# Four raw weight buffers, one down-projection buffer and a gather that skips padding rows in the experts of a two-layer decoder

## The reference, cut to what matters

```python
    gi = jnp.argmax(lg, axis=-1)
    ...
    top_p, top_i = lax.top_k(jax.nn.softmax(le, axis=-1), TOP_K)
    gate = p_top * top_p / jnp.sum(top_p, axis=-1, keepdims=True)
    ...
    def run_block(args):
        xb, e = args
        hid = jax.nn.silu(xb @ w_gate[e]) * (xb @ w_up[e])
        return hid @ w_down[e]
    ...
    y = jax.ops.segment_sum(out[dest] * sw[:, None], stok, num_segments=T)
```

## Time and profile before

| | |
|---|---|
| median of 3 runs | 3122.04 us (3121.51 to 3127.49) |
| profiled execution | 3119.75 us, span 3117.8 us |
| granted TensorE clock, mean | 0.936 of full speed |
| expert stage of layer 0, first to last gate/up product | 496.9 us, 47 blocks |
| expert stage of layer 1, the same | 485.1 us, 46 blocks |

### The profile page before, as it was taken

How to read it: one execution, slowest core, us unless ns; L and a number is a source line. 1 busy time by engine, 2 the same in 40 slices (tenths; PEclk the granted TensorE clock), 3 DMA queues, 4 the chain that set the end, 5 groups by cost and what they waited for, 6 DMA issues and landing times. The chain is left out here.

```text
span 3117.8 us, 48627 instructions
## 1 busy us (share of the span) xinstructions
PE 2673.4 (86%) x15109; PEld 2236.8 (72%) x15112; DVE 1747.1 (56%) x3154; ACT 1260.4 (40%) x2369; POOL 724.0 (23%) x923
## 2 busy tenths in 40 slices
PE   5999979997968947998898599799879947989997
PEld 4999958875847836777676488578658836767775
DVE  4222246665755665667765366588733354676664
ACT  3222132225841104556654222288611104675653
POOL 1000023321110002444343143211100002444433
PEclk9999989998988968999999799899979968999998
DMA  6111112215536516899997322222154415999995
GB/s 243 50 56 52 40 60 78 75 65 165 163 121 234 194 61 216 261 301 302 316 281 228 118 87 80 91 83 88 53 198 143 149 39 179 298 359 285 283 308 132
DMA packets 175389, 509.57 MB, mean 163 GB/s; under 512 B 53800, under 2 KB 81456, under 8 KB 150320
## 3 DMA queue, kind: packets, MB, share of 16 engines
q1 hardware_dynamic: 142480, 393.69, 34.7%
q0 software_dynamic: 32800, 114.51, 15.4%
HBM read 374.56 MB, written 133.56 MB: 163 GB/s over the span
## 5 line engine op out<-in xcount | busy, mean ns | idle before, releaser
L1700 DVE TENSOR_TENSOR moe_parts<-expert_w,moe_parts 128x1024 fp32r<-128x1024 f32 x384 | 452.3, 1221 | 238.4 <-ACT moe_parts L1649 234.9
L1582 PE MATMUL ps<-moe_parts,moe_xT 128*128 128x512 f32 x2232 | 551.6, 403 | 23.0 <-issue 16.0
L1582 PEld LDWEIGHTS ps<-moe_parts,moe_xT 128*128 128x128 f32 x2232 | 418.1, 191 | 125.3 <-issue 20.5
L1649 ACT ACTIVATE moe_parts<-expert_w 128x1024 fp32r<-128x1024 f32 x384 | 373.3, 1047 | 80.3 <-PEq L155 78.8
L1109 PE MATMUL ps<-out_w,out_catT 128*128 128x512 f32 x1344 | 322.4, 399 | 14.2 <-DVE out_w L1265 11.8
L560 PE MATMUL ps<-in_gate_w,in_gate_hnT 128*128 128x384 f32 (+1 forms) x1536 | 319.4, 367 | 7.4 <-DVE in_gate_w L679 7.4
L1582 PE MATMUL ps<-moe_parts,moe_hidT 128*128 128x512 f32 x1116 | 289.0, 408 | 26.9 <-DVE moe_hidT L1713 24.2
L560 PEld LDWEIGHTS ps<-in_gate_w,in_gate_hnT 128*128 128x128 f32 x1536 | 278.7, 190 | 37.4 <-issue 7.5
L1109 PEld LDWEIGHTS ps<-out_w,out_catT 128*128 128x128 f32 x1344 | 255.7, 192 | 69.4 <-DVE out_w L1265 12.6
L560 PE MATMUL ps<-in_qk_w,in_qk_hnT 128*128 128x512 f32 x1152 | 268.4, 394 | 9.2 <-DVE in_qk_w L679 9.2
L1582 PEld LDWEIGHTS ps<-moe_parts,moe_hidT 128*128 128x128 f32 x1116 | 205.7, 191 | 76.2 <-DVE moe_hidT L1713 32.8
(11 more groups left out here) (262 smaller groups left out, 4150.8 us busy)
## 6 DMA issues: line engine op xcount, KB each, us to landing
expert_w<-in_w_gate SPq DMA_DIRECT2D x64, 1024.0 KB
expert_w<-in_w_up SPq DMA_DIRECT2D x64, 1024.0 KB
expert_w<-in_w_down SPq DMA_DIRECT2D x64, 1024.0 KB
hn_d<-out_hn SPq DMA_DIRECT2D x32, 512.0 KB, 2.6
in_gate_xt<-in_x SPq DMA_DIRECT2D x16, 512.0 KB
in_qk_xt<-in_x SPq DMA_DIRECT2D x16, 512.0 KB
att_k<-k_d SPq DMA_DIRECT2D x64, 128.0 KB, 2.9
out_ht<-in_x SPq DMA_DIRECT2D x16, 512.0 KB, 4.6
```

Source lines behind the costliest of these rows:

```text
L1582: last = nc.tensor.matmul(out, left[:, a, k, :], right(b, k), start=(n == 0 and k == 0), stop=(n == 2 and k == K_ - 1))
L1649: nc.scalar.activation(parts[:, j, 0, at], K.expert_w[:, j, at], ACT.Copy).then_inc(w_high.sem, 1)
L1700: nc.vector.tensor_tensor(parts[:, j, 1, at], K.expert_w[:, j, at], parts[:, j, 0, at].bitcast(F32), ALU.subtract).then_inc(w_low.sem, 1)
```

## The change

- `RING` = 4 raw buffers: the two slots of `K.expert_w` and two more (`more`), with a semaphore each. Experts 2 and 3 are loaded at the start of the stage without a wait; expert e is loaded into the buffer of e - 4. w_gate waits for 2 gate/up pieces of e - 4, w_up for 4, w_down for its 2 down pieces.
- `parts` becomes `gu_parts` (two slots) and `d_parts` (one), with counters of their own. The down pieces of an expert are split at the end of its own first block, not at the end of the first block of the expert before. TensorE waits for `d_low` before every `lower`, and no longer for all pieces at the end of a first block.
- `pair` becomes `round_`: four experts are unrolled, in a loop of 6 rounds.
- The gather takes its rows from `K.where`, in which padding has a row number of 2048 or more, with a bounds check at 2047 that skips such rows. `xg` is cleared once before the first gather. `K.who` is gone.
- ScalarE reads the gate from `K.gates` directly; `set_gate` is gone.
- `w_in_odd` waits for 30 experts instead of 32.

```diff
+RING = 4
...
-            self.who = keep("who", [P, NBMAX], I32)
...
-                load_expert(K, sp, layer, e, e)
+                load_expert(K, sp, layer, e, K.expert_w[:, e, :], K.expert_in[layer][e])
...
-            own_.mark(V.tensor_copy(K.who[:, :], found[:, 1, :]))
...
-        gate = sb("gate", [P, 1])
-
-        parts = sb("parts", [P, 2, 2, EW], F32R)
+        more = sb("more", [P, RING - 2, EW])
+        ring = [K.expert_w[:, i, :] for i in range(2)] + [more[:, i, :] for i in range(RING - 2)]
+        gu_parts = sb("gu_parts", [P, 2, 2, GU], F32R)
+        d_parts = sb("d_parts", [P, 2, EW - GU], F32R)
         gathered_s, scattered_s = sem("gathered"), sem("scattered")
         who_set, where_set = Count(sem("who_set")), Count(sem("where_set"))
         x_turned, x_high, x_low = Count(sem("x_turned")), Count(sem("x_high")), Count(sem("x_low"))
-        w_high, w_low = Count(sem("w_high")), Count(sem("w_low"))
+        gu_high, gu_low, d_high, d_low = (sem(n) for n in ("gu_high", "gu_low", "d_high", "d_low"))
...
-            def pair(i, is_first, is_last):
-                for j in range(2):
-                    e = i * 2 + j
+            def round_(i, is_first, is_last):
+                for j in range(RING):
+                    e = i * RING + j
                     m0 = 0 if is_first and j == 0 else end_of(eng, e)
-                    first_block(i, j, m0, not (is_first and j == 0), not (is_last and j == 1))
+                    first_block(i, j, m0, not (is_first and j == 0), not (is_last and j == RING - 1))
                     end = end_of(eng, e + 1)
                     with eng.If(end > m0 + 1):
 
                         with eng.Fori(m0 + 1, end) as m:
-                            block(m, j)
-            pair(0, True, False)
-            with eng.Fori(1, NE // 2 - 1) as i:
-                pair(i, False, False)
-            pair(NE // 2 - 1, False, True)
+                            block(i, j, m)
+            round_(0, True, False)
+            with eng.Fori(1, NE // RING - 1) as i:
+                round_(i, False, False)
+            round_(NE // RING - 1, False, True)
...
-                load_expert(K, sp, layer, i * 2 + j, j, lambda n: alone(
-                    sp, w_low, i * (2 * PIECES) + ((j - 2) * PIECES + (n + 1) * PIECES // 3), K.tick_sp))
-            with sp.Fori(1, NE // 2) as i:
-                for j in range(2):
+                load_expert(K, sp, layer, i * RING + j, ring[j], K.expert_in[layer][j], lambda n: alone(
+                    sp, (Count(gu_low), Count(gu_low), Count(d_low))[n],
+                    ((i - 1) * RING + j) * (GU_PIECES, GU_PIECES, D_PIECES)[n] + (GU_PIECES // 2, GU_PIECES, D_PIECES)[n], K.tick_sp))
+            for j in range(2, RING):
+                load_expert(K, sp, layer, j, ring[j], K.expert_in[layer][j])
+            with sp.Fori(1, NE // RING) as i:
+                for j in range(RING):
                     load(i, j)
             if layer == 0:
 
-                sp.wait_ge(w_low.sem, NE * PIECES)
+                sp.wait_ge(gu_low, (NE - RING + 2) * GU_PIECES)
+                sp.wait_ge(d_low, (NE - RING + 2) * D_PIECES)
                 sp.dma_start(K.w_in_odd, K.x["w_in_odd"].rearrange("a (p k) n -> p (a k) n", k=DK)).then_inc(K.weights_in[5], 16)
 
         @block.gpsimd
         def _(g):
             def gather(m):
-                nc.gpsimd.tensor_copy(who[:, :], K.who[:, m:m + 1] if isinstance(m, int) else K.who[:, bass.ds(m, 1)]).then_inc(who_set.sem, 1)
+                nc.gpsimd.tensor_copy(who[:, :], K.where[:, m:m + 1] if isinstance(m, int) else K.where[:, bass.ds(m, 1)]).then_inc(who_set.sem, 1)
                 alone(g, who_set, m + 1, K.tick)
                 nc.gpsimd.indirect_dma_start(xg[:, :], None, K.hn_d[layer],
-                                             bass.IndirectOffsetOnAxis(ap=who[:, :], axis=0)).then_inc(gathered_s, 16)
-
-            def set_gate(m):
-                nc.gpsimd.tensor_copy(gate[:, :], K.gates[:, bass.ds(m, 1)]).then_inc(gated.sem, 1)
...
+            g.memset(xg[:, :], 0.0).then_inc(cleared, 1)
+            g.wait_ge(cleared, 1)
             gather(0)
...
-                set_gate(m - 1)
-
                 alone(g, x_turned, m + 2, K.tick)
                 gather(m + 2)
                 scatter(m - 1)
-            set_gate(total - 1)
...
-                pe.wait_ge(w_low.sem, i * (2 * PIECES) + j * PIECES + GU_PIECES)
+                pe.wait_ge(gu_low, i * (RING * GU_PIECES) + (j + 1) * GU_PIECES)
                 raise_(m, j)
                 turn_x(m + 1)
                 if behind:
-                    lower(m - 1, 1 - j)
-                pe.wait_ge(w_low.sem, i * (2 * PIECES) + (j + 1) * PIECES)
-                pe.sem_inc(K.tick_pe, 1)
-
-            def block_(m, j):
+                    pe.wait_ge(d_low, i * (RING * D_PIECES) + j * D_PIECES)
+                    lower(m - 1)
+
+            def block_(i, j, m):
                 turn_hid(m - 1)
                 raise_(m, j)
                 turn_x(m + 1)
-                lower(m - 1, j)
+                pe.wait_ge(d_low, i * (RING * D_PIECES) + (j + 1) * D_PIECES)
+                lower(m - 1)
             turn_x(0)
             in_turn(pe, first_block, block_)
             total = end_of(pe, NE)
             turn_hid(total - 1)
-            lower(total - 1, 1)
+            pe.wait_ge(d_low, NE * D_PIECES)
+            lower(total - 1)
...
-            def split(i, j, pieces):
-
-                for n in pieces:
+            def split_gu(i, j):
+                a.wait_ge(K.expert_in[layer][j], i * 48 + 48)
+                for n in range(GU_PIECES):
                     at = slice(n * PIECE, (n + 1) * PIECE)
-                    nc.scalar.activation(parts[:, j, 0, at], K.expert_w[:, j, at], ACT.Copy).then_inc(w_high.sem, 1)
+                    nc.scalar.activation(gu_parts[:, j % 2, 0, at], ring[j][:, at], ACT.Copy).then_inc(gu_high, 1)
+
+            def split_d(j):
+                for n in range(D_PIECES):
+                    at = slice(n * PIECE, (n + 1) * PIECE)
+                    nc.scalar.activation(d_parts[:, 0, at], ring[j][:, GU + n * PIECE:GU + (n + 1) * PIECE], ACT.Copy).then_inc(d_high, 1)
...
-                until(a, gated, m + 1)
-
                 a.wait_ge(scattered_s, m * 16 + 16)
-                nc.scalar.activation(y[:, :], yp, ACT.Copy, scale=gate[:, 0:1]).then_inc(y_out.sem, 1)
+                nc.scalar.activation(y[:, :], yp, ACT.Copy, scale=K.gates[:, bass.ds(m, 1)]).then_inc(y_out.sem, 1)
 
             def first_block(i, j, m, behind, ahead):
-                ni, nj = i + j, 1 - j
                 if ahead:
-
-                    a.wait_ge(K.expert_in[layer][nj], ni * 48 + 48)
                     if behind:
                         until(a, up, m)
-                    split(ni, nj, range(GU_PIECES))
+                    split_gu(i + (j + 1) // RING, (j + 1) % RING)
                 act(m)
                 x_out(m + 1)
                 if behind:
                     y_scaled(m - 1)
-                if ahead:
-                    split(ni, nj, range(GU_PIECES, PIECES))
-
-            def block_(m, j):
+                    split_d(j)
+
+            def block_(i, j, m):
                 act(m)
                 x_out(m + 1)
                 y_scaled(m - 1)
-            a.wait_ge(K.expert_in[layer][0], 48)
-            split(0, 0, range(PIECES))
+            split_gu(0, 0)
             x_out(0)
+            split_d(0)
...
+                ni, nj = i + (j + 1) // RING, (j + 1) % RING
                 if ahead:
-                    split(ni, nj, range(GU_PIECES // 2))
+                    split_gu(ni, nj, range(GU_PIECES // 2))
                 if behind:
                     hid_out(m - 1)
                 if ahead:
-                    split(ni, nj, range(GU_PIECES // 2, GU_PIECES))
+                    split_gu(ni, nj, range(GU_PIECES // 2, GU_PIECES))
                 hidden(m)
                 x_out(m + 1)
-                if ahead:
-                    split(ni, nj, range(GU_PIECES, PIECES))
-
-            def block_(m, j):
+                if behind:
+                    split_d(i, j)
+
+            def block_(i, j, m):
                 hid_out(m - 1)
                 hidden(m)
                 x_out(m + 1)
-            split(0, 0, range(PIECES))
+            split_gu(0, 0, range(GU_PIECES))
             x_out(0)
+            split_d(0, 0)
...
```

More of the change, by code:

```diff
@@ L175, in build @@
             self.weights_in = [self.ctx.enter_context(nc.semaphore(f"weights_in{i}")) for i in range(8)]
-            self.expert_in = [[self.ctx.enter_context(nc.semaphore(f"expert_in{l}{i}")) for i in range(2)]
+            self.expert_in = [[self.ctx.enter_context(nc.semaphore(f"expert_in{l}{i}")) for i in range(RING)]
                               for l in range(2)]
@@ L1283, in _, with load_expert @@
             log(end.plus(1))
-def load_expert(K, sp, layer, e, slot, until_free=lambda n: None):
```

(19 more changed lines are left out.)

14 lines of the change are left out of this document (7 added, 7 removed).

## The result

The changed kernel took 3162.2 us (median of 4 runs, 3155.2 to 3169.9), the kernel before 3122.3 beside it: a ratio of 1.0125, with a 95% interval of 1.0097 to 1.0152. The change makes the kernel slower by 40 us; forecast were +19 and 3139 us, inside a range of 3090 to 3172. The profiled execution took 3155.2 us with a span of 3153.5, 35.7 over that of before; it is the fastest of the four, so the trace shows 36 of the 40 us. The same stage can differ by some 10 us between the traces of two kernels whose medians agree (485 and 496 us for layer 1 in the kernel before and in `e4_shift`), so single traces are read here for mechanisms more than for their sums.

The account below looks back on a forecast made before the run. The prediction took the DMA engines, at nine tenths in the two expert stages, as the full resource. Its terms, 14 - 11 + 20 + 12 - 5 - 7 - 4 = +19 us on 3119.75, gave 3139 us, range 3090 to 3172.

Parts of the forecast that it names:

- (1): Start of each expert stage: memset, 6 MB loaded ahead of the first gather, next gathers delayed; +14 us (6 to 16).
- (2): Two-block expert after two-block expert: the 1.2 us stall goes, the gather inside the burst is short; -11 us (-13 to 0).
- (3): One-block expert after a two-block one: the gather falls behind the burst and comes late; +20 us (0 to 29).
- (4): First blocks after one-block experts, and runs of those: gathers take 8.90 us and come last; +12 us (-10 to +24).
- (5): Loop ends: rounds of four experts halve VectorE's waits before its splits; -5 us (-10 to 0).
- (6): w_in_odd load: last gather's rows all skipped, load two experts earlier meets a gather of 2 rows; -7 us (-9 to +4).
- (7): Last two experts of a layer run with no loads beside them; -4 us (-6 to 0).
- (8): Gate copies leaving GpSimd, removed table copy, single pair of w_down halves, bounds check on gathers: taken as 0.
- C: Gathers: a skipped row costs as much as a moved one; +57 us, 3177 us, chance 0.08.
- A: Gathers: the burst costs them nothing because skipped rows shorten it; -32 us, 3088 us, chance 0.25.
- D: Loop body of four experts no longer stays in the instruction store; fetches cost 54 to 107 us, about 3200, chance 0.04.
- B: Gathers behind the burst land at about 8.1 us, by turns between queues; -4 us, 3116 to 3124, chance 0.17.

Follow-up runs that it names:

- e4_shift: Kernel before with one unused tile of 224 bytes per partition ahead of the stages' tiles, shifting later addresses; 0.9993 of the kernel before.
- e3_late: Changed kernel with the loads of experts 2 and 3 held back until TensorE has turned the first block; 1.0110 of the kernel before, 3159.7 us.
- e1_paced: Changed kernel with SyncE loading in two portions, gate and up of expert e+1, then down of expert e; 3121.4 us, 0.9997 of the kernel before.
- e7_all_three: Changed kernel with two-portion loads, experts 2 and 3 held back until the first turn, and w_in_odd in four parts; 3109.2 us, 0.9946 of the kernel before.
- e2_all_rows: Changed kernel with the gather's bound above every index and hn_d 128 rows longer, so padding rows are fetched in full; 1.0173 of the kernel before.

## Why the prediction was right in its sign and half in its size

The sign and the mechanism held: the three loads go together because the wait for w_down queues gate and up behind it, the gather of the second block of a pair falls behind them, and undoing that alone returns the kernel's time. Step by step, from the table:

**(1) Start, +14: measured +14.4.** The parts were different. `e3_late` puts 4.9 us a layer on the 6 MB (4.4 were said) and leaves 2.3 for the memset and the bounds check (0.95 were said). I had also 1.5 us for the next gathers; they were not late. The chain of waits of layer 1 has the gather, for 4.51 in the earlier trace rows:

```profile
2605.96 10.26 DMA moe_xg<-hn_d,moe_who
```

**(2) Two-block behind two-block, -11: measured +2.7.** This is the step that failed. The stalls in second steps went, 127.1 to 112.7. But I called the gather issued in the burst "short", since some 25 rows of 128 are left of it. It was the gather of 50 rows, of 92 and of 2 that stalled TensorE for 2.25, 2.39 and 1.92 us, and the first steps grew from 115.1 to 132.2. A skipped row keeps its packet, and the packets have to get past the loads.

**(3) One-block behind two-block, +20: measured +31.7.** Eleven places with a stall of 1.8 us were said; of the 13 steps eleven do have one, 2.2 us each, 24.4 in all. The gather falls 3.1 us behind the first of the three issues, where I had 4.2 (my own rows give 9.53 + 1.8 - 7.54 = 3.8), and takes 9.4 us on average, not 8.9 less something for skipped rows. The other 7.3 us are what a stall does behind itself, which I hadn't counted. Columns as in the earlier trace rows: first what follows the 1.92 us stall of expert 5, then the 2.25 us one of expert 4:

```profile
1297.40:1301.30 3.90, 3.90 (x22) 3.40 (x23) 1.62 (x3) 1.03 (x1) 1.32 (x3) 1.00 0.38 77
...
1274.80:1280.30 5.50, 5.47 (x22) 4.77 (x23) 1.59 (x3) 1.02 (x1) 1.45 (x3) 0.69 0.49 95
```

The same 22 matmuls: at a granted clock of 1.00 (2.4 GHz) in 3.90 us, and at 0.69, between the levels of 2.4 and 1.2 GHz, in 5.50. A step costs its stall and 0.25 us, or its stall and 1.5 to 2.0 us: the latter in 6 of the 25 first steps behind two-block experts (and in expert 30's), all with stalls of 2.25 us or more, though one of 2.39 us cost no more than its 0.25. The granted clock goes with it: from the stall to the next product it is 0.65 to 0.73 in all seven, and 1.00 behind the stalls of 2.39, 2.17, 2.05 and 1.92 us. 6 x 1.5 = 9 us over those two kinds of step, which none of my terms had priced.

**(4) and (5) First blocks behind one-block experts, +12 and -5: measured about -5.** I said that a gather of 8.9 us would come last in the runs of one-block experts, a hair behind VectorE. It comes a hair ahead. 18 of these 33 gathers have all three loads issued in the 6 us before them, and TensorE takes them up 9.2 us behind their issue, yet hardly one stalls it: the waits fell from 21.9 to 1.5 us, and TensorE stands ahead of `lower` instead, so that the rows are there when it comes to turn them. The steps stayed at 12.0 us, since VectorE sets the pace, for which I had worked out 11.1. `lower` waits for the halves of the hidden values, which stand behind two gate/up splits:

```profile
2786.14 0.33 SPq L1293 DMA_DIRECT2D moe_more<-in_w_up  x1
...
2788.26 2.35 DVE L1700 TENSOR_TENSOR moe_gu_parts<-moe_more,moe_gu_parts 128x1024 fp32r<-128x1024 f32 x2
2788.44 3.00 PE L1582 MATMUL ps<-moe_d_parts,moe_hidT 128*128 128x512 f32 x12 [0.71 <-issue]
2789.05 1.36 POOL L1541 DMA_INDIRECT moe_xg<-hn_d,moe_who  x1 [0.89 <-POOL moe_who L1539]
...
2797.87 1.16 PE L1590 MATMUL ps<-ident,moe_xg 128*128 128x128 f32 x8
...
2799.37 0.42 DVE L1720 TENSOR_TENSOR moe_hidT<-ps,moe_hidT 128x256 fp32r<-128x256 f32 x1
2799.71 1.22 DVE L1700 TENSOR_TENSOR moe_gu_parts<-expert_w,moe_gu_parts 128x1024 fp32r<-128x1024 f32 x1
2799.90 0.47 PE L1582 MATMUL ps<-moe_d_parts,moe_hidT 128*128 128x512 f32 x1 [0.87 <-issue]
```

From `lower` to `lower` 11.46 us; the gather, 2.9 us behind the last of its three loads, is turned 8.8 us behind its issue without a stall. A gather that is no longer late gives nothing here; the waits ahead of `lower` in these 33 steps went from 22 to 48 us.

**(6) w_in_odd, -7: measured 0.** The end stall of 8.9 us is gone, and expert 30's first step grew by 9.1. I had it meet "one gather of 2 rows"; it did, and the 2 rows took 14.4 us. The same error as in (2).

**(7) Last two experts, -4: measured -1.3**, of which 0.5 is the shorter undisturbed step of (8). Their transfers had hardly been in the way before.

**(8) Gates, table, single down buffer, bounds check: 0.** No wait of `lower` for the down halves shows, and the bounds check adds 0.15 us to a gather's issue (1299 for 1154 ns on average): near nothing, but not for the first. Not foreseen: the matmuls' 3 ns (0.13 us in an undisturbed step, 12 us at most over 91 steps, all inside the sums above), and 4.0 us ahead of layer 0's stage and 2.8 between the layers, which lie within what such stretches vary from trace to trace (layer 0's stage starts at 1183.7 in `e1_paced`, at 1188.7 in `e7_all_three`, between which nothing ahead of it differs).

Sum: 14.4 + 2.7 + 31.7 - 4.9 + 0.2 - 1.3 - 4.0 - 2.8 = 36.0, against 35.7 in the spans. Of the 17 us by which it passes my +19, 14 are (2), 12 are (3), 7 are (6) and 3 are (7), all on the slow side; (4) and (5) give back 12, and what lies outside the stages 7. Without what they give back the time would have been some 3174 us, outside my range: that the range held is in part luck.

**The rivals.** C said that a skipped row costs as much as a moved one, 3177 us. Its mechanism is right in the larger part, and it got 0.08: q0 keeps its packets, the stalls in (2) are 15.0 us where C had 20, and (6) is 0. In bytes a skipped row does save something behind a burst, the 15 us between 3162 and `e2_all_rows`; that this run is at C's number (3177.0) isn't by C's terms, whose stalls in (2) were 20 us where it has 24.4. A, that skipping makes the burst harmless, is refuted by the same gathers.

D: the fetches on q8 went from 59 to 69 over the whole run. The two expert stages have 3 and 4 of them before and 8 and 10 now, none in the middle rounds (between 1337.6 and 1669.3 us, and between 2757.9 and 3079.8), and `e1_paced`, with the same 69, loses nothing. The Trainium skill's bound for the loop body (Runtime: NRT & Kernel Launch, "Instruction fetch mechanics"), a store of 2048 instructions for TensorE and 512 for the others, agrees with this trace.

B said that a backlog doesn't add. It does: the gathers that stalled TensorE took 9.2 us from issue to turn on average (the one at w_in_odd apart), for 8.2 before, and one with no row to fetch 15.3 us behind 5 MB. But it doesn't add in full. The first gather of layer 1's stage, with 6 MB of loads issued since 2603.44, has landed at 2616.22 (10.26 us), while these six loads still pass until 2621: it didn't wait for them to be through. B came from the rule of turns between queues, a packet each, in the Trainium skill (DMA: Bandwidth & Descriptors, "Queues, rings and completion order"). This gather agrees with turns being taken, but that a backlog should then not add was my inference, and it failed. The profile's packet records list rows of 4096 bytes, expert loads in packets of 8192 and w_in_odd in packets of 40960 (10240 in the four parts of `e7_all_three`, where the stall is gone). A turn behind larger packets would be longer, which fits the 15.3 us; no run changes their size alone, so this is not shown, nor that the profile's packets are those of the rule.

## What to carry to other kernels

When a wait is moved in front of other issues of the same queue, write down what then leaves together: here one `wait` on SyncE turned three spaced loads into a 3 MB burst, and 40 us hung on it, while the buffers were blameless. Price a small indirect gather by what stands in the queues ahead of it first and by its rows second: skipping rows saves bytes and keeps packets. And give a stall two prices, itself, and itself plus the stretch at a lower clock behind it.

## What the runs showed of the hardware that I had not expected

A gather whose every row is skipped took 15.3 us behind a 5 MB load; a skipped row is a packet of 4 bytes in place of 4096. The first bounds-checked gather of a stage took 2.06 us to issue, later ones 1.06. TensorE's granted clock behind a stall of 2.25 us was 0.69, behind one of 1.92 us 1.00; over the other steps the two kinds overlap a little, with 1.00 behind one of 2.39 us and 0.69 behind one of 2.32. And matmuls come every 229 instead of 232 ns once GpSimd no longer copies a gate for each block and ScalarE reads it in place, for which I have no mechanism.
